# Keeping weight tiles in memory between two token blocks of a fused block kernel

## What is computed

```
y   = concat(heads) @ attn_w_out               # output projection; h = h + gate * y
q   = (norm(h) @ w_query)                      # 16 column tiles of 128: 8 heads x 2 halves
s   = q . sub_keys ; top 16 x 16 -> 16 experts for each token and head
act = gelu(sum(u[expert] * norm(h)))           # u, v: rows of 1024, gathered from memory
h   = h + gate * sum(softmax(best) * act * v[expert])
a   = norm(h) @ w_pw1 + b                      # pointwise: 16 column tiles of 128
a   = a[:d] * sigmoid(a[d:]); a = depthwise conv, 31 taps; a = silu(layer_norm(a)) @ w_pw2
```

## Time and profile before

| | |
|---|---|
| time, median of 3 runs | 2917.06 us (2916.26 to 2918.3) |
| the profiled execution, its own time | 2914.11 us |
| its span | 2912.3 us |
| mean granted TensorE clock | 0.851 |
| TensorE busy | 2208.2 us (76%) |
| VectorE busy | 1875.5 us (64%) |
| ScalarE busy | 1247.1 us (43%) |
| GpSimd busy | 660.0 us (23%) |
| read from memory | 852.73 MB, 293 GB/s over the span |

### The profile page before, as it was taken

One profiled execution on the slowest core, in us unless ns is written; L12 is line 12 of the kernel. 1 busy time (PEld: TensorE's weight loads), 2 busy tenths in 40 slices (PEclk: granted clock), 3 DMA queues, 4 the chain that ended last, 5 costly groups with the idle time before them and its releaser, 6 DMA issues. The chain is left out here.

```text
span 2912.3 us, 41900 instructions
## 1 busy us (share of the span) xinstructions
PE 2208.2 (76%) x14298; PEld 1575.6 (54%) x14298; DVE 1875.5 (64%) x4128; ACT 1247.1 (43%) x3036; POOL 660.0 (23%) x600
## 2 busy tenths in 40 slices
PE   7988855544487667766443445999999999999998
PEld 4533733311175445544210112998759989985798
DVE  1886366667669556966776675667645666575555
ACT  3245233323357435653223333445444454464544
POOL 0420134444434333334444441000000000000000
PEclk9998977765599897888655555999999999999999
DMA  9970699999999999999999997555335545542554
GB/s 307 385 286 1 220 419 419 419 420 420 421 418 404 398 417 418 406 400 410 419 421 421 421 420 296 189 184 167 109 101 185 184 159 187 185 159 73 158 183 149
DMA packets 159308, 855.89 MB, mean 294 GB/s; under 512 B 17712, under 2 KB 17840, under 8 KB 92720
## 3 DMA queue, kind: packets, MB, share of 16 engines
q0 software_dynamic: 85392, 579.38, 48.4%
q1 hardware_dynamic: 72000, 261.73, 26.5%
q10 hardware_dynamic: 1760, 12.75, 1.3%
HBM read 852.73 MB, written 1.05 MB: 293 GB/s over the span
## 5 line engine op out<-in xcount | busy, mean ns | idle before, releaser
L2257 DVE TENSOR_TENSOR w_lo<-weights,w_hi 128x512 fp32r<-128x512 f32 x528 | 364.2, 691 | 281.1 <-ACT w_hi L988 279.1
L910 POOL DMA_INDIRECT arena<-experts,arena x308 | 365.1, 1185 | 650.3 <-PE ps L1862 442.5
L1862 PE MATMUL ps<-arena 128*32 128x512 f32 x1232 | 232.2, 838 | 347.7 <-ACT arena L1192 335.0
L988 ACT ACTIVATE w_hi<-weights 128x512 fp32r<-128x512 f32 x528 | 333.0, 632 | 375.7 <-PE ps L1814 278.9
L2510 DVE SCALAR_TENSOR_TENSOR arena<-arena 128x1024 f32<-128x1024 f32 x308 | 372.7, 1225 | 185.9 <-DMA arena<-experts,arena 180.1
L1812 PE MATMUL ps<-a_hi,w_hi 128*128 128x256 f32 x1408 | 399.8, 284 | 5.9 <-DVEq L2276 2.8
L1813 PE MATMUL ps<-a_lo,w_hi 128*128 128x256 f32 x1408 | 399.1, 283 | 0.0
L1814 PE MATMUL ps<-a_hi,w_lo 128*128 128x256 f32 x1408 | 399.1, 283 | 0.0
L1186 ACT ACTIVATE arena<-arena 128x1 f32<-128x1 f32 x512 | 101.7, 199 | 614.4 <-DVE arena L2510 348.2
L2510 DVE SCALAR_TENSOR_TENSOR held<-held,arena 128x1024 f32<-128x1024 f32 x204 | 247.1, 1223 | 111.9 <-DMA held<-experts,arena 106.3
L1862 PE MATMUL ps<-held,arena 128*32 128x512 f32 x816 | 157.3, 854 | 211.9 <-ACT arena L1192 210.8
(11 more groups left out here) (277 smaller groups left out, 3810.8 us busy)
## 6 DMA issues: line engine op xcount, KB each, us to landing
weights<-stream SPq DMA_DIRECT2D x497, 512.0 KB
arena<-mod_rows_in POOLq DMA_DIRECT2D x69, 512.0 KB, 8.6
mod_rows<-mod_rows_in POOLq DMA_DIRECT2D x11, 512.0 KB, 8.7
arena<-experts,arena POOLq DMA_INDIRECT x308
held<-experts,arena POOLq DMA_INDIRECT x204
arena<-gain_rows ACTq DMA_DIRECT2D x1, 3072.0 KB, 12.5
arena<-rpb_windows ACTq DMA_DIRECT2D x4, 512.0 KB, 13.6
arena<-keys_in ACTq DMA_DIRECT2D x2, 1024.0 KB, 9.3
```

The lines of the kernel that those rows point to most:

```text
L910: pool.indirect_dma_start(out=pair_of(k), out_offset=None, in_=experts[k // PICKS], in_offset=bass.IndirectOffsetOnAxis(ap=expert[:, at:at ...
L988: act.activation(w_hi[:, o % 2, part], weights[:, t.unit, part], ACT.Copy).then_inc(hi_ready, 1)
L1862: ins = pe.matmul(ps[first:first + WAVE, v % 2, :], diag[:, one % DIAGS, :], v_of(one, HALF * half, HALF * (half + 1)), start=(k % WAVE_PI ...
L2257: dve.tensor_tensor(w_lo[:, o % 2, part], weights[:, t.unit, part], w_hi[:, o % 2, part].bitcast(F32), ALU.subtract) \
```

## The change

The output projection's eight tiles are loaded once, with one DMA of 4.19 MB, into `held`, from a new input `kept_in`. Both `out` and `late` read them there. GpSimd's pick 6, the first that goes into `held`, waits for `late` 7. `late` moves to beats 0 to 3 on TensorE (two at each) and 2 to 5 on VectorE, and its norm to beats 7 to 11. Query tiles 9 to 15 of layer 0 are loaded once into seven kept places (parts of `arena` and of `mod_rows`) and used for both token blocks. Block 1's queries move to beats 16 + 3m. Later two of the seven places take the two pointwise tiles of chunk 7, loaded once for both convolution blocks. `pad` moves to beat 80, since the kept tiles lie in its place until then. To make room, `cand`, `cand2` and `eq` share one place, and so do `folded` and `y_wave`. SyncE issues the kept loads where the stream has come to their first use (`plan.marks`).

```diff
+KEPT = 7
+KEPT_QUERIES = list(range(9, 16))
+KEPT_AT = 23777
+KEPT_GLU = [7]
+LATE_BEAT = 0
...
     for m in range(KC):
-        put("late", m, pe=1 + m, dve=6 + 5 * (m // 4))
-    put("late_squares", 0, act=12)
-    put("late_norm", 0, pe=13, act=14, dve=15)
-    put("shift_late", 0, act=16)
+        put("late", m, pe=LATE_BEAT + m // 2, dve=LATE_BEAT + 2 + m // 2)
+    put("late_squares", 0, act=LATE_BEAT + 7)
+    put("late_norm", 0, pe=LATE_BEAT + 8, act=LATE_BEAT + 9, dve=LATE_BEAT + 10)
+    put("shift_late", 0, act=LATE_BEAT + 11)
     for m in range(2 * H):
-        put("query", 0, 1, m, pe=20 + 4 * m, act=21 + 4 * m)
+        put("query", 0, 1, m, pe=16 + 3 * m, act=17 + 3 * m)
     put("late_mods", 0, dve=22)
-    put("pad", 0, dve=24)
+    put("pad", 0, dve=80)
...
-    a["t_out"] = plan.tiles(8)
-    a["out"] = [plan.product(t) for t in a["t_out"]]
+    plan.marks.append((plan.index, "out"))
+    a["out"] = [plan.product() for _ in range(KC)]
...
+            if what == "query" and step[1] == 0 and step[3] in KEPT_QUERIES:
+                if step[2] == 0:
+                    plan.marks.append((plan.index, step))
+                tiles = [Kept(KEPT_QUERIES.index(step[3]), 1)]
+            elif what == "pw1" and step[2] in KEPT_GLU:
+                if step[1] == 0:
+                    plan.marks.append((plan.index, step))
+                tiles = [Kept(2 * KEPT_GLU.index(step[2]) + e, 2) for e in range(2)]
...
+        lasting = [arena[:, T * NKEY - D * (i + 1):T * NKEY - D * i] for i in range(3)]
+        kept = lasting[0:2] + [mod_flat[:, D:2 * D], lasting[2]] + \
+            [arena[:, KEPT_AT + D * i:KEPT_AT + D * (i + 1)] for i in range(3)]
...
+            for at, step in plan.marks + [(n_tiles, None)]:
+                run_loads([x for x in plan.loads if first <= x[2] < at])
+                first = at
...
+                if step == "out":
+                    sp.dma_start(held[:, :, :], kept_in[0:KC].rearrange("m p n -> p m n")).then_inc(held_loaded, 16)
+                elif step[0] == "query":
+                    i = KEPT_QUERIES.index(step[3])
+                    if i == 0:
+                        sp.wait_ge(row_dot, MOD_ROWS)
+                        wait_product(sp, PL["attn"]["O", H - 1])
+                    keep(i, KC + i)
+                else:
+                    for e in range(2):
+                        i = 2 * KEPT_GLU.index(step[2]) + e
+                        wait_product(sp, PL["gather", 0]["query", 0, 1, KEPT_QUERIES[i]])
+                        keep(i, KC + KEPT + i)
...
                     if k >= PAIR_RING:
                         pool.wait_ge(v_used, k - PAIR_RING + 1)
+                    if k == ARENA_PAIRS:
+                        wait_product(pool, PL["gather", 0]["late", KC - 1])
...
+            def out_columns(m, dst, tokens):
+                pe.wait_ge(held_loaded, 16)
+                for k in range(KC):
+                    ins = pe.matmul(dst, held[:, m, k * P:(k + 1) * P], oT[:, k, tokens], start=(k == 0), stop=(k == KC - 1))
+                return ins
...
                 def pad(_):
                     half = TAPS // 2
+                    wait_product(dve, pl["query", 0, 1, KEPT_QUERIES[-1]])
...
                     if v:
-                        wait_product(act, pl["fold", v - 1])
+                        wait_taken(act, pl["fold", v - 1])
```

More of the change, by code:

```diff
@@ L148, in __init__ @@
         self.bank_set = STREAM_BANKS
+        self.marks = []
     @staticmethod
@@ L410, in make_plan @@
                 if step[1] % 4 == 0:
-                    late = plan.product(late_tiles[step[1] + 3])
+                    late = plan.product()
                 a[step] = late
@@ L418, in make_plan @@
             else:
-                a[step] = plan.product(tiles[-1] if tiles else None)
+                a[step] = plan.product(tiles[-1] if tiles and isinstance(tiles[-1], Use) else None)
             plan.bank_set = WORK_BANKS
@@ L830, in load, with run_loads @@
                              stream[bass.ds(index, 1)].rearrange("o p n -> p o n")).then_inc(slot_loaded[slot], 16)
[L832 to L849, removed]
+            def run_loads(loads):
+                k = 0
+                while k < len(loads):
+                    if isinstance(loads[k][0], list):
+                        uses, times, first = loads[k]
+                        with sp.Fori(0, times) as i:
+                            for q, u in enumerate(uses):
+                                load(u.unit, i * u.per + (u.first - 1), i * len(uses) + (first + q))
+                        k += 1
+                        continue
+                    run = 0
+                    while (k + run < len(loads) and not isinstance(loads[k + run][0], list)
+                           and loads[k + run][0] == (loads[k][0] + run) % SLOTS):
+                        run += 1
+                    groups = run // SLOTS
+                    if groups > 1 and loads[k][1] == 1:
+                        for q in range(SLOTS):
+                            slot, use, index = loads[k + q]
+                            load(slot, use - 1, index)
+                        k += SLOTS
+                        run -= SLOTS
+                        groups -= 1
+                    if groups > 1:
+                        with sp.Fori(0, groups) as i:
+                            for q in range(SLOTS):
+                                slot, use, index = loads[k + q]
+                                load(slot, i + (use - 1), i * SLOTS + index)
+                        k += groups * SLOTS
+                        run -= groups * SLOTS
+                    for q in range(run):
@@ L862, in _, with keep @@
[L862 to L865, removed]
+                    k += run
+            def keep(i, row):
+                sp.dma_start(kept[i], kept_in[row]).then_inc(kept_loaded[i], 16)
+            first = 0
+            for at, step in plan.marks + [(n_tiles, None)]:
+                run_loads([x for x in plan.loads if first <= x[2] < at])
+                first = at
+                if step is None:
+                    continue
+                if step == "out":
[11 more added lines that the diff above has]
+                        keep(i, KC + KEPT + i)
@@ L1553, in loaded, with used @@
             def loaded(t, i=0):
-                pe.wait_ge(slot_loaded[t.unit], 16 * value(t, i))
+                if isinstance(t, Kept):
+                    pe.wait_ge(kept_loaded[t.at], 16 * t.load)
+                else:
+                    pe.wait_ge(slot_loaded[t.unit], 16 * value(t, i))
+            def used(ins, t, pr=None):
+                if not isinstance(t, Kept):
+                    ins.then_inc(tile_done[t.unit], 1)
+                elif pr is not None:
+                    finish(ins, pr)
             def finish(ins, pr):
@@ L2948, in gather @@
                 if what == "query":
[L2949 to L2952, removed]
+                    if which[0] or which[2] not in KEPT_QUERIES:
+                        put(column_tile(w["peer_w_query"][which[0]], which[2]))
+                elif what == "pw1" and which[1] not in KEPT_GLU:
                     put(column_tile(w["conv_w_pw1"][0], which[1]))
```

62 lines of the change are left out of this document (27 added, 35 removed).

## The result

| | before | after |
|---|---|---|
| median of 20 runs | 2915.81 us (2911.87 to 2924.63) | 2923.32 us (2913.56 to 2934.08) |
| ratio after / before, 95% interval | | 1.0022 [1.0014, 1.003] |
| the profiled execution, its own time | 2914.11 us | 2919.37 us |
| its span | 2912.3 us | 2917.6 us |
| mean granted TensorE clock | 0.851 | 0.843 |

The kernel became slower by about 6.4 us (0.0022 of 2916; the interval is 4 to 9), though it moves 8.9 MB less. The forecast was 2916.0, no change. The result lies inside the range of 2903 to 2927 and outside "within 0.2%", on the side of rival C.

A forecast was written before the change was run, and what follows sets the result against it. The prediction took DMA bytes at 0.415 MB per us to bound the middle part, from the picks to the feed-forward stages. Its terms -29.0 + 22 + 6 summed to -1.0 us, giving 2916 us, range 2903 to 2927.

The forecast's parts named there:

- within 0.2%: Whole kernel: the case that the time stays the same, 2911 to 2921 us, chance 0.39.
- rival C: Start of the picks: pick 6 waits longer for `late` 7; at a 32 us gap +9, 2926 us; chance 0.23.
- Part 1, the bytes: DMA-bound stretch after the first pick: 23 fewer tiles read, at 1.26 us each, -29.0 us.
- the four slots then refill ... before 350: Stream before the first pick: after the kept loads, four slots refill with block 1's first queries before 350 us.
- Part 2, the added wait: Start of the picks: pick 6 waits for `late` 7 and the DMA runs dry, +22 us (18 to 27).
- Part 3, the load in attention: Modulation rows: the 4.19 MB load delays VectorE's row dots and the end of attention, +6 us (0 to 10).
- The cover of 4 us: Attention: VectorE's waits for ScalarE and between the `head_apply` instructions hide about 4 us of the delayed row dots.
- Rival A: Attention: the 4.19 MB load is free; sum -7.0, 2910 us; chance 0.35 shared with other faster cases.
- Part 4, costs of nothing: Output stage, later block 1 queries, `pad`, `fold`, `choose` and the kept loads' wait: all covered, no cost.

The follow-up runs named there:

- best: Changed kernel with load_waits' wait, the eight `late` products between block 0's queries 7 and 8, `choose` 1 behind pick 3: 2892.68 us, again 2891.06 us.
- no_pointwise: Changed kernel, but the two pointwise tiles of chunk 7 are streamed again for both blocks: 2920.89 us, ratio 1.0011 to the kernel before.
- best_no_pointwise: best, but the pointwise tiles of chunk 7 are streamed for both blocks: 2893.44 us, ratio 0.9911 to the kernel before.
- late_first: Changed kernel, but TensorE's eight `late` products stand ahead of all beats, no pick pair between them: 2909.14 us, ratio 0.9972 to the kernel before.
- load_waits: Changed kernel, but the 4.19 MB load is held back until the last modulation row dot: 2908.15 us, ratio 0.9975 to the kernel before.
- best_early_load: best without the wait, so the 4.19 MB load goes out amid the modulation rows again: 2902.83 us, ratio 0.9951 to the kernel before.
- before_shared: Kernel before with only the new placement: shared places, `fold`'s longer wait, `pad` at beat 80: 2916.26 us, ratio 0.9995.
- held_only: load_waits with no stream tile kept, only the output projection loaded once: 2923.94 us, ratio 1.0032 to the kernel before.

## Why the prediction was wrong

**Part 1, the bytes: this term failed, by its size.** It said -29.0 us: 23 tiles at 1.26 us, 21 of them before pick 104 and 2 pointwise ones later. The price holds (1.27 us). The count does not. Up to the first pick the kernel before moves 234 GB/s x 349.5 us = 81.8 MB, after 237 x 353.4 = 83.8 MB: after is ahead by 3.8 tiles, where the forecast counted six (23 less the 17 that are gone altogether). The step was "the four slots then refill ... before 350". The seven kept loads and four refills are indeed issued from 337.94 to 348, but eleven tiles need 14 us, and two more before they flow; the stretch from 350 to 355 still moves 409 GB/s. The tail is in flight when the picks begin, and shares their time. From pick 0 to pick 160 the DMA moves 9.5 MB less than before (170.9 against 180.4), or 18.1 tiles, which at 420 GB/s is 22.6 us. The times say the same: 430.8 us of which 23.7 are empty, against 431.4 with 1.7, is 407.1 against 429.7, a saving of 22.6 us; best shows 23.0. The other part, -2.5 for two pointwise tiles, is not seen: the bytes are gone (409.0 MB from pick 160 to pick 511 against 410.4), but that stretch takes 2.4 us longer in after, and no_pointwise and best_no_pointwise point opposite ways. Whether the saving is hidden, cancelled by something or lost in a spread of 8 us stays open. Instead of -29.0 the term was about -23.

One reading of the page was off, without effect on the sum: the slice with a DMA digit of 6 and 220 GB/s is the fifth, so the saturated part is slices 6 to 24, and it moves 398 to 421 GB/s, not 380 to 421.

**Part 2, the added wait: right.** Forecast +22, bounds 18 to 27. Measured 23 us of empty DMA (371 to 394); by the shortfall to 420 GB/s 23.7, that is 22.0 more than before, and 19 to 22 in the other executions with this order of `late`. Each step is in the trace: the first pick pair comes 22.2 us behind pick 0 (20.7 forecast: 370.2 - 349.5; 20.2 in the second execution of after), `late` 2 to 5 in 9.34 us (9.8), pair 2 in 1.07, `late` 6 and 7 in 3.84. late_first and best show that an empty us is a lost us.

**Part 3, the load in attention: right in kind, a little small.** Forecast +6 (0 to 10), measured +7 to +9 in the profiles; the medians of load_waits and best_early_load say 10 to 14, at or beyond the upper bound. The rows came 2.72 us apart instead of 2.56. The cover of 4 us was there: `head_apply` ran back to back behind the late rows, as written. Rival A (free) is refuted by load_waits and best_early_load.

The Trainium skill ("DMA: Bandwidth & Descriptors", section Issuing engines are not separate DMA queues) says that transfers started by different engines run on the same 16 DMA engines and interleave. The trace agrees: SyncE's one load halves the pace of GpSimd's rows (2.72 against 1.28 us).

**Part 4, costs of nothing: right** (before_shared, 0.9995). From pick 104 to 160 every changed kernel is 1.5 us longer (145.2 against 143.6). This is no cost: no stream load is issued there in either kernel and the DMA moves 420 to 421 GB/s in both, only 61.0 MB instead of 60.4. About half a pick's bytes pass on the other side of the issue of pick 104.

**Sum.** With what the profiles gave, -22.6 + 22.0 + 6.9 = +6.3, against the measured +6.4 (4 to 9). The forecast said -1.0. Nearly all of the miss is term 1 (6.4 us too much: 2.9 tiles fewer than counted up to pick 160, and the two pointwise tiles), the rest the load in attention (0.9). That the sum meets the measured time to 0.1 us is luck: the profiles spread by several us at the start and behind pick 160, and there the terms say nothing. Rival C had the sign and nearly the time (2926), but not the reason: the gap was 22 to 24 us, not 32. Three terms of 6 to 29 us left a sum near zero, and an error of a fifth in the largest was enough to turn it.

## What to carry to other kernels

- Saved bytes count only if they leave the stretch that the DMA limits. Count them by the megabytes moved up to the event at which that stretch begins, in both kernels, and not by the tiles already issued. In the same way a gap is measured by the DMA's GB/s and not by how long the queue's owner waits: held_only waits longer for pick 6 than load_waits (31.9 us against 29.6) and has less emptiness (19.0 against 21.3).
- A buffer that is shared with the first stage of a full DMA ring adds a wait at the worst place. Ask what the ring's owner now waits for and move that work ahead of the ring's start (best, which also holds the early load back, takes 31 to 32 us less than after by the medians, for the same bytes; its reordering was run as a whole).
- One big early load is not free where small ones feed an engine one by one. Hold it back with one wait until they are through, if its user is far away.

## What the runs showed that I had not expected

- The same instructions take different times in the long stretch of picks 160 to 511: load_waits 988.8 and 994.7 us, and 989.1 to 997.2 over the other kernels, while two executions of the kernel before agree within 0.2 us there. The start, up to the first row dot, varies from 61.4 to 68.8. Only medians of many runs carry a verdict of 0.2%.
- ScalarE was once idle for 5.14 us ahead of a copy with a releaser given as `remote`, its matmuls recorded as done some 2 us before (360.1 against 362.00); in the kernel before has 5.49 us of the same. There SyncE's next load is issued at 363.99, with the copy at 363.86, which suggests that the product really ended then and that the record of its matmuls is too early. It wasn't tested.
- The 4.19 MB load took 26.7 us to land among the rows; a kept tile in `arena` took 10.2 us in the median, with 1.26 us of bytes in it.
